# Hybrid encoder trunk: the first two experts' rows come from one-hot products behind the output projection, and the second expert has no gather

## The chip, the cores and the metric

The kernel runs on one core of a Trainium2 chip. The metric is the time of one launch in microseconds on the device. Three runs of the kernel before gave 1538.98, 1540.01 and 1540.28 us.

## The reference

Two layers work on 512 tokens of 1024 numbers in float32. Each layer adds a mixer (eight heads of attention with a forget gate, four heads of retention, then an output projection) and a mixture of experts, and a last RMS norm ends the program. The expert part is what this case is about:

```python
g_idx = argmax(g_logits)                      # one of 4 groups
top_v, top_i = top_k(e_in_group, 2)           # two of its 8 experts
weights = g_w * softmax(top_v)
a = silu(xblk @ w_expert_gate[e]) * (xblk @ w_expert_up[e])
yb = a @ w_expert_down[e]                     # 32 experts, 1024 -> 512 -> 1024
out = segment_sum(yb * w_buf[:, None], tok_buf)
```

Each of the 32 experts has 6.3 MB of weights, so a layer reads some 200 MB for its experts, whatever the tokens choose.

## The kernel before, in words

Each engine has its own program, and the programs meet at semaphores. Up to the router, `steps(layer)` writes out the order of the work by hand, as a list of tuples that PE, ACT and DVE each walk through, doing their own part of each step. `banks()` gives each step a PSUM bank. SP only issues loads of weights; POOL writes the normalised rows to DRAM and issues the gathers.

At the end of the list stands the output projection of four tiles of 128 tokens (t = 0 to 3) in two halves, as `("wp", t, 1, part)` and `("wo", t, half)`. Between its matmuls stand small steps. `fT` transposes half of a tile's residual rows and ACT or DVE copies them from PSUM. `lg` multiplies them with the router weights, and behind its second half DVE runs `choose(layer, t)`: 14 operations, each waiting for the one before, that find the best group, the best expert and the second best, and write a row of `chosen`. `rank` is a product on PE with a triangular matrix that gives each token its place within its expert, which DVE copies and turns into `hot_first`, a one-hot over 64 slots for expert 0. `xb` multiplies this one-hot with the normalised rows `xn2`: the result, in bank 3, are the rows of expert 0, both halves of the width side by side on 64 + 64 partitions. `count` counts the tokens of each expert. `unread` products are written and not read.

Then come 32 experts in a ring of three weight slots. An expert has a gate and an up product (L1774, 32 instructions each), a gated product on DVE, a transpose (L1783), a down product (L1790) and the "spread" (L1750), a one-hot product that adds the weighted results to the tokens and of which DVE adds each part to the residual rows (L1143). The rows of experts 1 to 31 are gathered by POOL from DRAM, by the table `gath`, which is made from `slots_by_expert` (L1486) within expert 0; they are transposed (L1742) within the expert before their own. DVE's `take_input(e)` weighs them with the norm's weights into `xT`. In expert 0 DVE also does `route`, `weigh` and `further`, for the tables.

SP's queue is in order. When the output projection's last step is through, it loads the down weights of expert 0 and up and down of expert 2 (the others are there already). Then it goes through experts 3 to 31: the gate weights wait for the gate product of the expert three before, the up weights for its up product, and the down weights for its down product.

Of the kernel before, what the change touches and what calls it, by code (L numbers as in the profile page):

```python
# [14 lines left out]
P = 128  # L15
# [154 lines left out]
def steps(layer):  # L170
# [62 lines left out]
    out += [("rank", 2), ("fT", 3, 1), ("xb", 2), ("lg", 3, 1), ("rank", 3), ("xb", 3), ("count",)]  # L233
# [7 lines left out]
def banks():  # L241

    acc, uses, where = 0, [0] * 8, {}
    for s in STEPS_OF[0] + [("more",)]:
# [5 lines left out]
        if kind in ("S", "V", "rv"):  # L250
            if kind == "S":
# [18 lines left out]
        elif kind == "RV":  # L270
            b = 6 + s[1] % 2
        elif kind == "RN":
            b = 4 + s[1] % 2
        elif kind == "lg":
            s, b = s[:2], (2, 3, 6, 7)[s[1]]
        elif kind == "fT":
            b = 4 + s[1] % 2
        elif kind in ("rank", "count"):
            b = 2
        elif kind == "xb":  # L280
            s, b = ("xb",), 3
# [20 lines left out]
def trunk_kernel(nc, x, norm_mix_w, w_in, fox_forget_b, w_out, norm_ffn_w, w_router_group, b_router_group,  # L302
                 w_router_expert, b_router_expert, w_expert_gate, w_expert_up, w_expert_down, norm_final_w,
                 const, rope, decay, number, out):
    with ExitStack() as ctx:
# [73 lines left out]
        xg = [at(start, 512) for start in (XF0, XG0, XG0 + 512)]  # L379
        xT = at(XT0, 512).rearrange("p (j h s) -> p j h s", j=4, h=2)  # L380
# [25 lines left out]
        lgt = at(RA0, NT * (NG + NE)).rearrange("p (a b) -> p a b", a=NT)  # L406
        chosen = split("chosen", RA0 + 144, [NT, NE])
        hot_first = [at(RA0 + 304 + t * SLOTS, SLOTS) for t in range(NT - 1)] + [rt(SLOTS)]
        in1, in2, pen, gfi = (at(RA0 + 496 + 4 * i, 4) for i in range(4))
        rank = at(RB2, NT * NE).rearrange("p (a b) -> p a b", a=NT)  # L410
        near, other, o1 = (at(RB2 + 128 + NE * i, NE) for i in range(3))
# [3 lines left out]
        gs = rt(NT, NG)  # L415
# [120 lines left out]
        def gathered(layer, e):  # L536

            count = [len(range(i or 3, NE, 3)) for i in range(3)]
            return 16 * (layer * count[e % 3] + e // 3 + (e % 3 > 0))
# [165 lines left out]
        def _(pool):  # L705
            for layer in range(DEPTH):
# [28 lines left out]
                is_full(pool, ("xb",), layer)  # L735
# [22 lines left out]
                pool.wait_ge(s_xtf, layer * NE + NE - 1)  # L758
# [23 lines left out]
        def _(act):  # L782
# [26 lines left out]
            for layer in range(DEPTH):  # L809
# [13 lines left out]
                for s in STEPS_OF[layer]:  # L823
# [145 lines left out]
                    elif kind == "fT" and s[2] == 0:  # L969
# [3 lines left out]
                                             ).then_inc(freed[b], 2)  # L973
                    if s in UNITS and UNITS.index(s) + CUT < NU:
# [8 lines left out]
                act.wait_ge(s_rin, 2 * layer + 1)  # L983
                nc.scalar.activation(ed, ed, ACT.Exp).then_inc(s_rexp, 1)
                act.wait_ge(s_rin, 2 * layer + 2)
# [43 lines left out]
        def _(dve):  # L1029
# [51 lines left out]
            def choose(layer, t):  # L1081

                g_log, e_log = lgt[:, t, 0:NG], lgt[:, t, NG:].rearrange("p (g e) -> p g e", g=NG)
                gm, top, second = (v[:, t:t + 1] for v in (gmax, m1, m2))
                i1, i2 = in1[:, t:t + 1], in2[:, t:t + 1]
# [12 lines left out]

                link(stt(out=near, in0=o1, scalar=NEG, in1=near, op0=ALU.mult, op1=ALU.add))
# [4 lines left out]
                    ).then_inc(s_hot, 1)  # L1104

            def first_rows(layer):

                for kth, found in enumerate((in1, in2)):
                    link(tt(a12f[:, kth, :, :], over(k("x"), NT), each(found, NE), ALU.is_equal))
                tt(ed, m2, m1, ALU.subtract).then_inc(s_rin, 1)  # L1110
                tt(gs, lgt[:, :, 0:NG], each(gmax, NG), ALU.subtract).then_inc(s_rin, 1)
# [70 lines left out]
            for layer in range(DEPTH):  # L1182
# [5 lines left out]
                for s in STEPS_OF[layer]:  # L1188
# [155 lines left out]
                    elif kind == "fT" and s[2]:  # L1344
# [5 lines left out]
                        if t == NT - 1:  # L1350
                            nc.vector.tensor_copy(wbig, each(nfe[:, layer, :].rearrange("p (h j) -> p j h", h=2), SLOTS))
                    elif kind == "lg" and s[2]:
# [5 lines left out]
                        nc.vector.scalar_tensor_tensor(out=lgt[:, t, :], in0=bank[b][:, 0:NG + NE],  # L1358
# [3 lines left out]
                        choose(layer, t)  # L1362
                    elif kind == "rank":
# [6 lines left out]
                        ts(hot_first[t], k("slot")[:, 0:SLOTS], rank[:, t, 0:1], chosen[:, t, 0:1].bitcast(F32),  # L1370
                           ALU.is_equal, ALU.mult).then_inc(s_first_hot, 1)
# [3 lines left out]
                def take_input(e):  # L1375
                    dve.wait_ge(s_xtf, layer * NE + e + 1)
# [99 lines left out]
        def _(pe):  # L1476
# [50 lines left out]
            for layer in range(DEPTH):  # L1527
                srow = layer * FH * NT
                for s in STEPS_OF[layer]:
# [5 lines left out]
                    elif kind == "xb":  # L1535
                        name, first = ("xb",), s[1] == 0
# [159 lines left out]
                    elif kind == "xb":  # L1696
                        t = s[1]
                        pe.wait_ge(s_xn2, NT * layer + t + 1)
                        pe.wait_ge(s_first_hot, NT * layer + t + 1)
# [7 lines left out]
                    elif kind == "xb":  # L1707
                        done = s[1] == NT - 1
# [22 lines left out]
                def first_transpose():  # L1731
                    b, n = result(("xb",), layer)
                    for j in range(4):
                        if j % 2 == 0:
                            pe.wait_ge(freed[b], 2 * n - 1 + j // 2)
                        last = tr(bank[0][:, P * j:P * (j + 1)], xg[0][:, P * j:P * (j + 1)], ident)
                    last.then_inc(s_xtf, 1)
# [28 lines left out]
                def gate_up(slot, before=None):  # L1766
# [30 lines left out]
                def expert(e):  # L1797
                    i, g = e % RING, layer * NE + e + 1
                    loads = 16 * (layer * per(i) + e // RING + 1)
                    pe.wait_ge(s_xt, g)  # L1800
# [8 lines left out]
                    gate_up(i, ahead).then_inc(s_gu, 1)  # L1809
                    if e == 0:  # L1810
                        weights_by_expert()
# [10 lines left out]
                    if e < NE - 1:  # L1822
# [76 lines left out]
```

## Time and profile before

| | |
|---|---|
| runs | 1538.98, 1540.01, 1540.28 us |
| profiled execution | 1543.27 us, its span 1541.2 us |
| PE, DVE, ACT, POOL busy | 97%, 54%, 24%, 17% of the span |
| mean granted clock of PE | 0.991 |
| HBM | 464.33 MB read, 305 GB/s over the span |

### The profile page before, as it was taken

To read this page: it belongs to the slowest core of one execution; us is meant where nothing else is said; L and a number is where in the kernel's file an instruction comes from. 1 tells how busy PE (TensorE), PEld (TensorE's weight loads), DVE (VectorE), ACT (ScalarE), POOL (GpSimd) and SP (SyncE) were. 2 spreads that over 40 slices of the span, in tenths; PEclk is the share of its full clock that TensorE was granted. 3 is DMA by queue.
4 is the path that set the end of the run, shared out by engine and by line. 5 is a ranking of instruction groups with operands and counts; after the bars stand their busy time and mean duration, and the time that the engine had idled before them with its cause. 6 is when DMAs were issued, how large, how long until landed. Compare 5 with 4: busy or idle time off the path is not lost. (4 is left out here: it accounts for less than half of the span.)

```text
span 1541.2 us, 23569 instructions
## 1 busy us (share of the span) xinstructions
PE 1487.8 (97%) x9368; PEld 931.0 (60%) x9368; DVE 829.7 (54%) x1592; ACT 368.3 (24%) x722; POOL 259.3 (17%) x153
## 2 busy tenths in 40 slices
PE   8999999999999999999999999998999999999996
PEld 6877767655555555545488777685555555554543
DVE  2267773645555555554624686625655555555456
ACT  6335463300000000000163354732000000000002
POOL 3342331110000000000133331501000000000001
PEclk9999999999999999999999999999999999999998
DMA  6442146589999999999833321467999999999995
GB/s 210 99 97 69 42 164 272 202 356 424 421 424 422 423 422 423 423 423 424 338 118 91 82 69 28 173 278 280 391 425 421 425 420 424 421 423 422 425 423 227
DMA packets 105773, 464.05 MB, mean 301 GB/s; under 512 B 16616, under 2 KB 59880, under 8 KB 72640
## 3 DMA queue, kind: packets, MB, share of 16 engines
q1 hardware_dynamic: 98208, 449.14, 73.0%
q0 software_dynamic: 6112, 12.32, 2.1%
q8 instruction: 78, 1.28, 0.3%
q10 hardware_dynamic: 1344, 1.05, 0.2%
q14 instruction: 31, 0.25, 0.0%
HBM read 464.33 MB, written 6.29 MB: 305 GB/s over the span
## 5 line engine op out<-in xcount | busy, mean ns | idle before, releaser
L1774 PE MATMUL bank<-area 128*64 128x256 f32 x4096 | 462.2, 382 | 15.4 <-DMA area<-in_w_expert_up_dram 12.5
L1774 PEld LDWEIGHTS bank<-area 128*64 128x64 f32 x4096 | 289.0, 137 | 182.9 <-issue 26.4
L1143 DVE TENSOR_TENSOR xres<-xres,bank 128x512 f32<-128x512 f32 x512 | 316.6, 681 | 5.3 <-PE bank L1750 5.3
L1790 PE MATMUL bank<-area 128*64 128x512 f32 x1024 | 238.0, 607 | 5.9 <-DVE area L1402 1.0
L744 POOL DMA_INDIRECT area<-rows,gath x62 | 69.9, 1127 | 732.9 <-PE bank L1742 700.0
L995 ACT ACTIVATE y_hi<-bank,slot_w 128x512 fp32r<-128x512 f32 x64 | 44.0, 688 | 586.5 <-PE bank L1790 586.5
L1380 DVE TENSOR_TENSOR area<-area,bank 128x256 f32<-128x256 f32 x64 | 27.0, 421 | 288.3 <-PE bank L1774 288.3
L717 POOL TENSOR_TENSOR w_lo<-area,w_hi 128x1024 fp32r<-128x1024 f32 x55 | 135.1, 2458 | 273.5 <-ACT w_hi L815 273.5
L1790 PEld LDWEIGHTS bank<-area 128*64 128x64 f32 x1024 | 68.9, 138 | 133.9 <-issue 113.3
L1596 PE MATMUL bank<-h_hi,w_hi 128*128 128x512 f32 x336 | 135.0, 402 | 0.0
L1601 PE MATMUL bank<-h_hi,w_lo 128*128 128x512 f32 x320 | 124.9, 390 | 0.0
L1600 PE MATMUL bank<-h_lo,w_hi 128*128 128x512 f32 x320 | 124.7, 390 | 0.0
L1750 PE MATMUL bank<-y_hi,onehot 64*128 64x512 f32 x512 | 115.5, 446 | 3.0 <-issue 1.6
L1750 PE MATMUL bank<-y_lo,onehot 64*128 64x512 f32 x512 | 102.3, 394 | 0.0
L1750 PEld LDWEIGHTS bank<-y_hi,onehot 64*128 64x128 f32 x512 | 48.4, 184 | 83.5 <-issue 75.8
L991 ACT ACTIVATE area<-bank 128x256 f32<-128x256 f32 x64 | 24.5, 383 | 261.5 <-PE bank L1774 261.5
L1384 DVE SCALAR_TENSOR_TENSOR y_lo<-bank,slot_w,y_hi 128x512 fp32r<-128x512 f32 x64 | 48.1, 751 | 62.9 <-ACT y_hi L995 62.8
L815 ACT ACTIVATE w_hi<-area 128x1024 fp32r<-128x1024 f32 x58 | 61.6, 1062 | 80.3 <-PE bank L1524 33.3
L1596 PEld LDWEIGHTS bank<-h_hi,w_hi 128*128 128x128 f32 x336 | 63.0, 188 | 22.9 <-issue 10.3
L1601 PEld LDWEIGHTS bank<-h_hi,w_lo 128*128 128x128 f32 x320 | 60.1, 188 | 13.0
L1600 PEld LDWEIGHTS bank<-h_lo,w_hi 128*128 128x128 f32 x320 | 60.1, 188 | 11.4
L1402 DVE COPY area<-bank 128x256 f32<-128x256 f32 x64 | 27.2, 425 | 67.8 <-PE bank L1783 67.5
(203 smaller groups left out, 1711.1 us busy)
## 6 DMA issues: line engine op xcount, KB each, us to landing
area<-in_w_expert_up_dram SPq DMA_DIRECT2D x64, 2048.0 KB, 25.8
area<-in_w_expert_gate_dram SPq DMA_DIRECT2D x64, 2048.0 KB, 23.5
area<-in_w_expert_down_dram SPq DMA_DIRECT2D x64, 2048.0 KB, 25.1
area<-in_w_in_dram SPq DMA_DIRECT2D x58, 512.0 KB, 3.9
area<-in_w_out_dram SPq DMA_DIRECT2D x4, 2048.0 KB, 11.0
rows<-area POOLq DMA_DIRECT2D x8, 512.0 KB, 3.2
area<-in_decay_dram SPq DMA_DIRECT2D x2, 1024.0 KB, 6.5
out_dram<-area SPq DMA_DIRECT2D x4, 512.0 KB, 2.9
```

The lines of the kernel that those rows point to most:

```text
L717: nc.gpsimd.tensor_tensor(w_lo[g % CUT][:, :, :], slab[g % RAW], w_hi[g % CUT][:, :, :].bitcast(F32), ALU.subtract).then_inc(s_wlo, 1)
L744: pool.indirect_dma_start(out=xg[e % 3], out_offset=None, in_=rows_dram, in_offset=bass.IndirectOffsetOnAxis(ap=gath[:, e:e + 1], axis=0), ...
L815: nc.scalar.activation(w_hi[g % CUT][:, :, :], slab[g % RAW], ACT.Copy).then_inc(s_whi, 1)
L995: nc.scalar.activation(y_hi[e % 2][:, :], bank[3][:, :], ACT.Copy, scale=slot_w[:, e:e + 1]).then_inc(s_yh, 1)
L1143: tt(xs, xs, bank[4 + i][:, :], ALU.add).then_inc(s_sa[i], 1)
L1384: return nc.vector.scalar_tensor_tensor(out=y_lo[e % 2][:, :], in0=bank[found][:, :], scalar=weight, in1=y_hi[e % 2][:, :].bitcast(F32), o ...
L1596: mm(o[:, :], hi[:, c, :], h_hi[:, c, :], start=(c == 0), stop=False)
L1600: mm(o[:, :], hi[:, c, :], h_lo[:, c, :], start=False, stop=False)
L1601: last = mm(o[:, :], lo[:, c, :], h_hi[:, c, :], start=False, stop=(c == KC - 1))
L1750: yield mm(bank[4 + 2 * (t % 2) + half][:, :], onehot[parity][rows, P * t:P * (t + 1)], part[rows, :], start=(w_ == 0), stop=(w_ == 1))
L1774: last = mm(bank[i][SLOTS * half:SLOTS * (half + 1), 0:256], xT[:, c % 4, c // 4, :], w[:, i, c, 256 * half:256 * (half + 1)], start=(c == ...
L1790: last = mm(bank[into][SLOTS * half:SLOTS * (half + 1), :], hx[:, c % 2, c // 2, :], w[:, c, 512 * half:512 * (half + 1)], start=(c == 0), ...
```

## The change

The one-hot of a tile now has 128 columns: 64 slots of expert 0 and 64 of expert 1. `xb` makes two products with it, one for each half of the width, into banks 3 and 6. All four `xb` steps now stand behind the output projection. DVE copies the first result and ACT the second into `two_rows`, four transposes turn each (banks 5 and 7), and `take_input(0)` and `take_input(1)` make their input from these banks, in two products of 256 columns each. Expert 0's gate product starts when the first is there, and waits for the second at its fifth chunk. Expert 1 has no gather and no transposes within expert 0, and POOL gathers expert 2 first, then 3 and 4 as soon as the first transposes are done. The slot table is made behind expert 0's up product, not ahead of it. `choose` is split into nine and five operations with one more (a subtraction for the softmax over groups, which was one operation for all tiles); for tile 2 the second part stands behind the copy of `fT(3, 1)`. `rank(2)` stands behind the last logits, one `unread` product is gone, and in the first part the logits of tiles 0 to 3 stand a step later. The buffers `lgt`, `near`, `o1`, `gs` share or change places.

The diff, cut to its core (the second places of buffers and the gathers' semaphore counts are left out):

```diff
-    out += [("wo", 0, 0), ("wo", 1, 0), ("fT", 0, 0), ("wo", 2, 0), ("fT", 1, 0), ("lg", 0, 0)]
-    out += [("wo", 3, 0), ("fT", 2, 0), ("lg", 1, 0)]
-    between = [[("fT", 3, 0), ("lg", 2, 0)], [("lg", 3, 0)], []]
+    out += [("wo", 0, 0), ("wo", 1, 0), ("fT", 0, 0), ("wo", 2, 0), ("fT", 1, 0), ("wo", 3, 0), ("lg", 0, 0), ("fT", 2, 0)]
+    between = [[("lg", 1, 0), ("fT", 3, 0)], [("lg", 2, 0)], [("lg", 3, 0)]]
     for t in range(1, NT):
-        between += [[("fT", t - 1, 1)],
-                    [("rank", t - 2), ("lg", t - 1, 1)] if t > 1 else [("lg", t - 1, 1)],
-                    [("xb", t - 2)] if t > 1 else []]
+        between += [[("fT", t - 1, 1)], [("rank", t - 2), ("lg", t - 1, 1)] if t > 1 else [("lg", t - 1, 1)], []]
     for n, small in enumerate(between):
         out += [("wp", n // 3, 1, n % 3), *small]
         if n % 3 == 2:
             out += [("wo", n // 3, 1)]
-    out += [("rank", 2), ("fT", 3, 1), ("xb", 2), ("lg", 3, 1), ("rank", 3), ("xb", 3), ("count",)]
+    out += [("xb", 0), ("fT", 3, 1), ("xb", 1), ("lg", 3, 1), ("rank", 2), ("rank", 3), ("xb", 2), ("xb", 3), ("count",)]
...
+                made = {0: [(("xb", 0), 3), (("xb", 1), 6)], 3: [(("xt", 0), 5), (("xt", 1), 7)]}.get(s[1], [])
...
-        hot_first = [at(RA0 + 304 + t * SLOTS, SLOTS) for t in range(NT - 1)] + [rt(SLOTS)]
...
+        hot_two = [at(start, 2 * SLOTS) for start in (RA0 + 216, RA0 + 344, RB2 + 128)] + [rt(2 * SLOTS)]
...
-                is_full(pool, ("xb",), layer)
+                is_full(pool, ("xb", 0), layer)
...
-                for e in range(1, RING):
-                    gather(e)
+                gather(2)
                 for e in range(RING, NE):
-                    pool.wait_ge(s_xtf, layer * NE + e - RING + 1)
+                    if e == RING:
+                        is_full(pool, ("xt", 0), layer)
+                    elif e - RING >= 2:
+                        pool.wait_ge(s_xtf, block_turned(layer, e - RING))
...
+                    elif s == ("xb", NT - 1):
+                        b, n = result(("xb", 1), layer)
+                        is_full(act, ("xb", 1), layer)
+                        nc.scalar.activation(two_rows[1], bank[b][:, :], ACT.Copy).then_inc(freed[b], 2)
...
+            def choose_second(layer, t):
...
+                ts(gs[:, t, :], lgt[:, 0:NG], gmax[:, t:t + 1], None, ALU.subtract).then_inc(s_rin, 1)
...
-                b, n = result(("xb",), layer)
-                is_full(dve, ("xb",), layer)
-                for half in range(2):
-                    own = slice(256 * half, 256 * (half + 1))
-                    nc.vector.tensor_copy(xg[0][:, own], bank[b][:, own]).then_inc(freed[b], 1)
+                b, n = result(("xb", 0), layer)
+                is_full(dve, ("xb", 0), layer)
+                nc.vector.tensor_copy(two_rows[0], bank[b][:, :]).then_inc(freed[b], 2)
...
+                            choose_second(layer, t - 1)
...
-                        choose(layer, t)
+                        choose_first(layer, t)
+                        if t != NT - 2:
+                            choose_second(layer, t)
...
-                        ts(hot_first[t], k("slot")[:, 0:SLOTS], rank[:, t, 0:1], chosen[:, t, 0:1].bitcast(F32),
-                           ALU.is_equal, ALU.mult).then_inc(s_first_hot, 1)
+                        for e in range(2):
+                            ts(hot_two[t][:, SLOTS * e:SLOTS * (e + 1)], k("slot")[:, 0:SLOTS], rank[:, t, e:e + 1],
+                               chosen[:, t, e:e + 1].bitcast(F32), ALU.is_equal, ALU.mult).then_inc(s_first_hot, 1)
...
+                    if e < 2:
+                        for h in range(2):
+                            b, n = result(("xt", h), layer)
+                            is_full(dve, ("xt", h), layer)
+                            found = bank[b][:, :].rearrange("p (j s) -> p j s", j=4)[:, :, SLOTS * e:SLOTS * (e + 1)]
+                            made = tt(xT[:, :, h, :], found, wbig[:, :, h, :], ALU.mult)
+                            if e == 0 or h:
+                                made.then_inc(s_xt, 1)
+                            else:
+                                link(made)
+                        if e:
+                            dve.wait_ge(s_xt, input_part(layer, e))
+                            for h in range(2):
+                                dve.sem_inc(freed[result(("xt", h), layer)[0]], 2)
+                        return
...
-                            last = mm(o[SLOTS * half:SLOTS * (half + 1), :], hot_first[t],
-                                      xn2[t][:, 512 * half:512 * (half + 1)], start=(t == 0), stop=(t == NT - 1))
+                            to = result(("xb", half), layer)[0]
+                            last = mm(bank[to][:, :], hot_two[t], xn2[t][:, 512 * half:512 * (half + 1)],
+                                      start=(t == 0), stop=(t == NT - 1))
+                            if t == NT - 1:
+                                last.then_inc(full[to], 1)
...
-                        unread(0, 512, 512, 512, 512)
+                        unread(0, 512, 512, 512)
...
+                        may_fill(pe, ("xt", h), layer)
+                        is_taken(pe, ("xb", h), layer)
+                        for j in range(4):
+                            last = tr(bank[b][:, P * j:P * (j + 1)], two_rows[h][:, P * j:P * (j + 1)], ident)
+                        last.then_inc(full[b], 1)
...
+                            if parts and i == 0 and c == 4:
+                                pe.wait_ge(s_xt, input_part(layer, 0))
...
-                        if part and e == 0:
-                            slots_by_expert()
...
+                        slots_by_expert()
                         weights_by_expert()
...
-                    if e < NE - 1:
+                    if 0 < e < NE - 1:
```

## Rows read from the trace of the kernel before

**Rows 1.** Windows of the expert phases: busy us by engine, clock, DMA share, GB/s.
```profile
321.00:329.00 8.00, 8.00 (x50) 3.71 (x48) 6.88 (x20) 0.72 (x2) 0.29 (x1) 0.78 0.43 120
329.00:760.00 431.00, 422.06 (x3122) 232.29 (x3120) 226.56 (x397) 33.77 (x62) 30.68 (x27) 1.00 1.01 422
...
1069.00:1072.00 3.00, 3.00 (x28) 2.09 (x26) 0.35 (x2) 0.38 (x1) 0.00 (x0) 1.00 0.54 104
...
1083.00:1088.00 5.00, 5.00 (x42) 2.81 (x40) 4.62 (x13) 0.90 (x2) 0.00 (x0) 1.00 0.65 191
```

**Rows 2.** SP's issues in time: start us, us, engine, line, operation.
```profile
291.63 0.38 SPq L607 DMA_DIRECT2D area<-in_w_expert_down_dram  x1
...
325.51 0.38 SPq L607 DMA_DIRECT2D area<-in_w_expert_down_dram  x1
...
1084.33 0.38 SPq L607 DMA_DIRECT2D area<-in_w_expert_down_dram  x1
```

**Rows 3.** PE in time, layer 0; in brackets idle before and releaser.
```profile
280.60 1.08 PE L1701 MATMUL bank<-area 128*64 128x512 f32 x4
...
284.51 0.60 PE L1674 MATMUL bank<-kst,xres 128*128 128x128 f32 x4
...
291.44 0.34 PE L1691 MATMUL bank<-chosen,sums 128*128 128x32 f32 x2
...
295.32 3.68 PE L1499 MATMUL bank<-kst 128*128 128x512 f32 x8
...
302.00 0.62 PE L1695 MATMUL bank<-chosen,sums 128*128 128x32 f32 x4
...
304.14 3.67 PE L1774 MATMUL bank<-area 128*64 128x256 f32 x32 [0.78 <-DVE area L1377]
...
312.35 1.97 PE L1493 MATMUL bank<-area,hot_slot 128*128 128x32 f32 x16
314.15 0.42 PE L1783 MATMUL bank<-kst,area 128*128 128x128 f32 x2
318.18 1.12 PE L1742 MATMUL bank<-kst,area 128*128 128x128 f32 x4 [3.61 <-DMA area<-rows,gath]
319.22 6.24 PE L1790 MATMUL bank<-area 128*64 128x512 f32 x16
...
335.37 3.65 PE L1790 MATMUL bank<-area 128*64 128x512 f32 x16
```

**Rows 4.** PE in time, the same place in layer 1.
```profile
1050.94 0.34 PE L1691 MATMUL bank<-chosen,sums 128*128 128x32 f32 x2
...
1060.49 1.08 PE L1701 MATMUL bank<-area 128*64 128x512 f32 x4 [0.84 <-DVE area L1370]
...
1064.07 5.88 PE L1774 MATMUL bank<-area 128*64 128x256 f32 x32 [0.79 <-DVE area L1377]
```

**Rows 5.** Windows of one microsecond, layer 1, columns as in Rows 1.
```profile
1061.00:1062.00 1.00, 1.00 (x8) 0.50 (x4) 0.55 (x4) 0.88 (x3) 0.29 (x1) 0.88 0.95 348
...
1068.00:1069.00 1.00, 1.00 (x10) 0.66 (x8) 0.00 (x0) 0.00 (x0) 0.00 (x0) 0.71 0.95 401
```

**Rows 6.** DVE in time, layer 0: choice, projection's add, one-hot, first 256-wide product.
```profile
282.68 0.25 DVE L1103 SCALAR_TENSOR_TENSOR chosen<-kst,area 128x32 fp32r<-128x32 f32 x1
283.39 0.69 DVE L1339 TENSOR_TENSOR xres<-xres,bank 128x512 f32<-128x512 f32 x1 [0.46 <-PE bank L1668]
...
299.17 0.25 DVE L1103 SCALAR_TENSOR_TENSOR chosen<-kst,area 128x32 fp32r<-128x32 f32 x1
...
300.53 0.32 DVE L1370 TENSOR_SCALAR area<-kst,area,chosen 128x64 f32<-128x64 f32 x1
...
304.00 0.41 DVE L1052 TENSOR_TENSOR area<-area 128x256 f32<-128x256 f32 x1
```

**Rows 7.** The page's table of DMA queues.
```profile
q0 software_dynamic: 6112, 12.32, 2.1%
```

**Rows 8.** The source view of the gathers, line 744.
```profile
DMA to landing us min/median/max: 3.9/8.2/11.0
```

More of the change, by code:

```diff
@@ L379, in trunk_kernel @@
         xg = [at(start, 512) for start in (XF0, XG0, XG0 + 512)]
+        two_rows = [at(XF0 + i * 512, 512) for i in range(2)]
         xT = at(XT0, 512).rearrange("p (j h s) -> p j h s", j=4, h=2)
@@ L404, in rt_one_pass @@
             return split(name, start, list(shape))
-        lgt = at(RA0, NT * (NG + NE)).rearrange("p (a b) -> p a b", a=NT)
-        chosen = split("chosen", RA0 + 144, [NT, NE])
-        hot_first = [at(RA0 + 304 + t * SLOTS, SLOTS) for t in range(NT - 1)] + [rt(SLOTS)]
-        in1, in2, pen, gfi = (at(RA0 + 496 + 4 * i, 4) for i in range(4))
+        chosen = split("chosen", RA0, [NT, NE])
+        lgt = at(RA0 + 128, NG + NE)
+        in1, in2, pen, gfi = (at(RA0 + 168 + 4 * i, 4) for i in range(4))
+        other = at(RA0 + 184, NE)
         rank = at(RB2, NT * NE).rearrange("p (a b) -> p a b", a=NT)
-        near, other, o1 = (at(RB2 + 128 + NE * i, NE) for i in range(3))
+        hot_two = [at(start, 2 * SLOTS) for start in (RA0 + 216, RA0 + 344, RB2 + 128)] + [rt(2 * SLOTS)]
+        near, gs = slot_w[:, 0:NE], slot_w[:, NE:NE + NT * NG].rearrange("p (a b) -> p a b", a=NT)
+        o1 = slot_tok[:, 0:NE]
+        assert NE + NT * NG <= NCOL
         gmax, m1, m2 = (stat[:, 20 + 4 * i:24 + 4 * i] for i in range(3))
@@ L536, in gathered, with block_turned, input_part @@
         def gathered(layer, e):
-            count = [len(range(i or 3, NE, 3)) for i in range(3)]
-            return 16 * (layer * count[e % 3] + e // 3 + (e % 3 > 0))
+            first = (RING, RING + 1, 2)[e % RING]
+            return 16 * (layer * len(range(first, NE, RING)) + (e - first) // RING + 1)
+        def block_turned(layer, e):
+            return layer * (NE - 2) + e - 1
+        def input_part(layer, e):
+            return layer * (NE + 1) + e + 2
         def spread_use(layer, e, t):
@@ L757, in _ @@
                 n_more = pool.value_load(ovn[0:1, 0:1], min_val=0, max_val=NOV)
-                pool.wait_ge(s_xtf, layer * NE + NE - 1)
+                pool.wait_ge(s_xtf, block_turned(layer, NE - 1))
                 with pool.If(n_more > 0):
@@ L1079, in slot_weights, with choose_first @@
                 dve.sem_inc(s_wt, 1)
[L1081 to L1085, printed above, removed]
+            def choose_first(layer, t):
+                g_log, e_log = lgt[:, 0:NG], lgt[:, NG:].rearrange("p (g e) -> p g e", g=NG)
+                gm, top, i1 = gmax[:, t:t + 1], m1[:, t:t + 1], in1[:, t:t + 1]
                 stt = nc.vector.scalar_tensor_tensor
@@ L1097, in choose @@
                 link(ts(o1, k("x"), i1, None, ALU.is_equal))
+            def choose_second(layer, t):
+                second, i2 = m2[:, t:t + 1], in2[:, t:t + 1]
+                stt = nc.vector.scalar_tensor_tensor
                 link(stt(out=near, in0=o1, scalar=NEG, in1=near, op0=ALU.mult, op1=ALU.add))
@@ L1357, in _ @@
                         dve.wait_ge(s_rstd2, layer * NT + t + 1)
-                        nc.vector.scalar_tensor_tensor(out=lgt[:, t, :], in0=bank[b][:, 0:NG + NE],
+                        if t:
+                            dve.wait_ge(s_rin, (NT + 1) * layer + t)
+                        nc.vector.scalar_tensor_tensor(out=lgt, in0=bank[b][:, 0:NG + NE],
                                                        scalar=stat[:, 16 + t:17 + t], in1=rtb[:, layer, :],
@@ L1535, in _ @@
                     elif kind == "xb":
-                        name, first = ("xb",), s[1] == 0
+                        name, first = ("xb", 0), s[1] == 0
                     elif kind == "begin":
@@ L1707, in _ @@
                     elif kind == "xb":
-                        done = s[1] == NT - 1
+                        done = False
                     elif kind in ("begin", "wp"):
@@ L1731, in first_transpose @@
                 def first_transpose():
[L1732 to L1737, printed above, removed]
+                    for h in range(2):
+                        b, n = result(("xt", h), layer)
+                        may_fill(pe, ("xt", h), layer)
[3 more added lines that the diff above has]
+                        last.then_inc(full[b], 1)
                 def input_transpose(e):
@@ L1764, in spread_block, with gate_up @@
                             made[2 + half].then_inc(s_sf[2 * (t % 2) + half], 1)
-                def gate_up(slot, before=None):
+                def gate_up(slot, before=None, parts=False):
                     w = wexp[slot][0]
@@ L1807, in ahead @@
                         pe.wait_ge(s_w[i][part], loads)
-                    gate_up(i, ahead).then_inc(s_gu, 1)
+                    gate_up(i, ahead, e == 0).then_inc(s_gu, 1)
                     if e == 0:
+                        slots_by_expert()
                         weights_by_expert()
```

22 lines of the change are left out of this document (10 added, 12 removed).

## The prediction

> **What bounds the kernel now.** I read first the windows over both expert phases. [rows 1] show the weight stream: once it runs it holds a DMA share of 1.01 and 422 to 423 GB/s, to 760 in layer 0 and alike in layer 1, which is the rate at which these phases end; PE is never short of work there by more than a little. So what a change ahead of the stream is worth is read from the stretches in which DMA isn't full: 321 to 329 (120 GB/s, so 8 x (1 - 120/422) = 5.7 us lost), 1069 to 1072 (104 GB/s, 2.3 us) and 1083 to 1088 (191 GB/s, 2.7 us). Then SP's issues [rows 2]: three loads go out from 291.63 on, when the output projection is through, the gate weights of expert 3 when expert 0's gate product ends (304.14 + 3.67, [rows 3]), and its down weights only at 325.51, when expert 0 has left its slot. From that issue nothing is dry again. Full rate comes some 1.9 us after an issue (effective start 327.4: 321 + 5.7, and 0.7 for the transfers of a gather that lie in this gap). Third, PE's order in time [rows 3] says why 325.51: PE starts expert 0 at 304.14 (I call this E0), has turned its hidden rows at 314.5, and then stands 3.61 us for the gathered rows of expert 1, after which the down product takes 6.24 us, against 3.65 us in the next expert, since the granted clock stood at 1.2 GHz. Layer 1 is 759.5 us later at the end of the output projection (1050.94 against 291.44), starts expert 0 at 1064.07 with a gate product of 5.88 us at 1.2 GHz, waits again for gathered rows, and issues down weights at 1084.33 [rows 2, 4, 5]. In both layers the distance E0 to this issue is long: 21.4 and 20.3 us.
>
> **The projection's end.** Two one-hot products (xb) leave it: one at 280.60 and one like it in the next tile, each 1.01 us and 0.1 us of waiting, 2.2 us of PE in all [rows 3]. DVE gives some back. The choice of a tile gets one more 4-wide subtraction (about 0.17 us), and the add of the projection stands behind it. At 283.39 this add waited 0.46 us for PE, with the choice over at 282.93; with two such subtractions ahead the choice ends at 283.3, and DVE becomes the bound there: the add comes at 283.3, so removing the first xb brings fT(2,1), four transposes, only from 284.51 to 284.15 [rows 3, 6]. From there PE is free: 0.36 + 1.11 = 1.5 us earlier, W = 289.95. DVE's choice there is cut after its ninth of 14 operations (2.1 us of 3.35) and ends at 289.7, just in time. Bounds: 0.4 us (the DVE keeps all else) and 2.2 us. The second expert's one-hot is one more 64-wide operation per tile, 0.32 us, 0.17 if it overlaps; DVE waits about that long for the next logits just behind it, which hides it; without that cover 0.3 us a tile [rows 6]. SP's three loads at 291.63 go out 1.5 us earlier as well. The logits moved behind wo(3,0) swap 0.9 us of PE work within a stretch in which no load is short; zero, and 0.3 us either way if not.
>
> **From W to E0.** An xb is now two products of 128 columns instead of two of 64. The trace has no such xb; the nearest row is the four unread 512-wide ones, 8 instructions in 3.68 us, so 0.92 us each, 1.84 us for a pair. The lower end is the 1.01 us of the pair of 64, the upper end twice 1.84 at the low clock; I take 1.84. PE then: xb(0) 289.95 to 291.9, fT(3,1) 0.4, xb(1) to 294.2, logits 0.92 to 295.15, three unread ones (2.76, one fewer) to 297.9, rank(2) 0.4. All of it but the logits' end at 295.15 is beside DVE's chain: the choice of tile 3 took from 295.32 (end of logits) to 299.42, 4.1 us [rows 3, 6], so it ends at 299.25. The five late operations of tile 2 (1.2 us) and the copy for the weights stand at 292.9 to 294.8, before the logits, in DVE idle time: no cost, but a price of up to 1.2 us if the logits come sooner. Then what was not there: DVE's subtraction, the copy of rank(2) and its release (0.6 us), since rank(3) uses the same bank. rank(3) 299.85 to 300.45; xb(2), xb(3) 3.7 us, which wait for four one-hots of 0.32 us made during rank(3), to 304.3; count 0.6; four transposes 0.4 (fT: the next work starts 0.35 after them); the first of two 256-wide products on DVE 0.42 [rows 3, 6] and 0.2 of signals: E0 = 305.7, against 304.14. The copy of the first half (0.69 us) lies beside the second half of xb(3) and the count; ACT's copy of the second half, if it takes as long, ends beside the count and the first transposes; the second product on DVE is needed 1.8 us after E0 and is done by then. The move puts 1.6 us onto E0; bounds 0 and 4.5 us. In layer 1 E0 = 1050.94 - 1.5 + 15.75 = 1065.2.
>
> **From E0 to the down weights.** Gate and up 7.2 us; the slot table, now behind both, 1.0; the weight table 1.85; hidden transposes and the copy back 1.1 (hidden transposes at 314.15; the same step takes that long in the next expert); down 3.65: 14.85 us, issue at 320.55 and 1080.05 [rows 3]. The wait for the gather is gone, and so is the low clock that followed it. DVE waits for the table at E0 + 8.3 ahead of its gated product; this ends at E0 + 9.2, and the weight table on PE runs until E0 + 10.05, which hides it. On POOL's queue gather(2) is now first, then 3 and 4 at once. gather(2) is issued at E0 + 9.6, lands 8.2 us later, at worst 11.0 [rows 8], so by E0 + 21.7, and PE asks for it at E0 + 24.4, one expert on: nothing waits. What is late next? The gate weights of expert 3: issued at E0 + 3.7, full rate at + 5.6, two loads 4.19 MB / 423 GB/s = 9.9 us and three gathers of 0.13 MB each (12.32 MB of this queue less 4.2 MB for the saved rows, over 62 [rows 7, 8]) 0.9 us: E0 + 16.4, against 14.85 + 1.9 = E0 + 16.75 for the down weights. So both end nearly together, and the down weights still decide.
>
> **Sum.** Layer 0: 325.51 - 320.55 = 4.95. Layer 1: 1084.33 - 1080.05 = 4.3. One gather fewer in a stream that is full: 0.13 MB, 0.3 us, twice. 9.85 us in all with the clock full. PE has the same 4.95 and 4.3 us, so its waits for weights don't grow.
>
> **The clock.** [rows 4, 5] against [rows 3]: with the same work the granted clock fell to 1.2 GHz at 1061.8 in layer 1 (the mean of that microsecond is 0.88), after waits of at most 0.84 us, and did not in layer 0. The fall lasted to 1068.6 and made the gate product 5.88 instead of 3.67 us and the transposes 0.3 longer: 2.5 us. After the change PE waits 1.5 us in one piece (298.3 to 299.85) at this place, in both layers, so I expect what the trace shows, a fall in one of two: 9.85 - 2.5 = 7.35. The Trainium skill (TensorE: Matmul & The Clock Gate, HAM oscillation) ties such falls to waits for data far longer than these; by that rule there is no fall ahead of E0 and the sum is 9.85. By that rule the fall at 1061.8 should not be there, so the trace doesn't agree.
>
> The profiled execution took 1543.27 us (span 1541.2 and 2.07 around it), 3.26 above the median 1540.01. 1543.27 - 7.35 = 1535.9 in its terms, 1532.7 in the median's.
>
> **Rivals.** (a) Forecast, 0.45: 1532.7. (b) No fall ahead of either E0, 0.27: 1540.01 - 9.85 = 1530.2. For: layer 0; against: longer wait than in layer 1. (c) A fall in both layers for the 6.8 us that it lasted at 1061.8 to 1068.6, each 3.4 us of lost work on products that fill PE: 9.85 - 6.8 = 3.05, 1537.0; 0.2. For: the wait is there in both; against: the 3.7 us of full products that follow it. (d) Slower, 0.08: PE stays at 1.2 GHz from W on, because four one-hot products of double width and only three unread ones change what the clock sees. The work from W to E0 on PE is 13.8 us, of which DVE's chain hides some 3: 10.7 us more per layer. Break-even is where E0 slips by 6.5 us in layer 0 (21.4 - 14.85) and 5.4 in layer 1, that is with 13 and 11 us of low clock; then 2 x 10.7 - 9.85 = 11.5 slower, 1551.6. Against: before W PE is full, and the longest fall seen ahead of experts is 6.8 us. (e) That the gain is hidden by another wait, as that for gather(2), needs a landing 2.7 us above the largest of 62; I fold it into (c).
>
> **Chances.** Some 0.2% (3.1 us) is what a measurement tells from no change. Half of (c) counts as within it: faster 0.82, within 0.12, slower 0.06. The range goes from (b) less the bounds of the projection's end (0.7 us in each layer), 1528.8, to (c) and half a microsecond, 1537.5; slower cases are left out.
>
> **What would show it.** Right: no wait for gathered rows in expert 0; down product 3.65 us there; last projection product 1.5 us sooner; E0 1.6 us later counted from the layer's start in layer 0; down weights of expert 3 out at 320.6 in layer 0; between 308 and 311 a new dry stretch of DMA of up to 3 us, and after 323 none. Wrong: E0 later than 308, an xb pair of more than 2 us at full clock, a wait at input_transpose(2), or a stream that is full as early as said and an end that does not follow it.

## The result, and the profile after

The changed kernel took 1530.94 us (median of 10 runs, 1529.91 to 1537.1), the kernel before 1540.32 in the same comparison (10 runs, 1538.98 to 1544.58): ratio 0.9941, 95% interval 0.9929 to 0.9952, so 9.1 us less, at least 7.4. A second comparison of the two gave 1532.53 (6 runs) against 1540.35, ratio 0.9942 (0.9928 to 0.9956). The forecast was 1532.7 within 1528.8 to 1537.5. The profiled execution took 1530.88 us, span 1529.0.

PE in time in layer 0, to be read beside [rows 3] (start us, us, engine, line, operation, idle before and its releaser):

```profile
287.60 1.88 PE L1739 MATMUL bank<-area 128*128 128x512 f32 x4
289.31 0.60 PE L1709 MATMUL bank<-kst,xres 128*128 128x128 f32 x4
289.75 1.88 PE L1739 MATMUL bank<-area 128*128 128x512 f32 x4
291.47 0.98 PE L1717 MATMUL bank<-rtw,area 128*128 128x36 f32 x8
292.28 2.82 PE L1534 MATMUL bank<-kst 128*128 128x512 f32 x6
...
296.52 0.51 PE L1726 MATMUL bank<-chosen,sums 128*128 128x32 f32 x3 [1.18 <-DVEq L1388]
...
297.24 3.67 PE L1739 MATMUL bank<-area 128*128 128x512 f32 x8
...
302.31 7.13 PE L1817 MATMUL bank<-area 128*64 128x256 f32 x64
...
313.15 3.65 PE L1833 MATMUL bank<-area 128*64 128x512 f32 x16 [0.67 <-DVE area L1437]
```

The wait for the gathered rows is gone, and the down product is 3.65 us. The projection's end, W, is where the first pair of 128-column products starts: 287.60 against 291.44. Expert 0's gate product, E0, starts at 302.31 against 304.14: earlier, where I had it 1.6 us later. Layer 1 ends its expert 0 otherwise:

```profile
1055.04 7.13 PE L1817 MATMUL bank<-area 128*64 128x256 f32 x64
1062.10 1.06 PE L1521 MATMUL bank<-hot_exp,hot_slot 128*128 128x32 f32 x8
1063.02 1.95 PE L1528 MATMUL bank<-area,hot_slot 128*128 128x32 f32 x16
1064.80 0.41 PE L1826 MATMUL bank<-kst,area 128*128 128x128 f32 x2
1065.89 6.67 PE L1833 MATMUL bank<-area 128*64 128x512 f32 x16 [0.67 <-DVE area L1437]
```

From the end of the projection up to the down product the granted clock is 1.00 in both layers; then the down product of layer 1 runs at 0.50, and takes 6.67 us where that of layer 0 took 3.65. SP's issues, beside [rows 2]:

```profile
287.79 0.38 SPq L615 DMA_DIRECT2D area<-in_w_expert_down_dram  x1
...
306.03 0.33 SPq L607 DMA_DIRECT2D area<-in_w_expert_gate_dram  x1
...
316.85 0.38 SPq L615 DMA_DIRECT2D area<-in_w_expert_down_dram  x1
...
991.96 0.34 SPq L607 DMA_DIRECT2D area<-in_w_expert_gate_dram  x1
...
1072.60 0.38 SPq L615 DMA_DIRECT2D area<-in_w_expert_down_dram  x1
```

And the windows of the stretches in which the stream is not full, in the columns of [rows 1]:

```profile
306.00:308.00 2.00, 2.00 (x22) 1.32 (x20) 0.50 (x2) 0.39 (x1) 0.00 (x0) 1.00 0.63 135
308.00:310.00 2.00, 2.00 (x20) 1.33 (x16) 0.00 (x0) 0.00 (x0) 0.00 (x0) 1.00 0.87 352
...
316.00:320.00 4.00, 4.00 (x36) 2.42 (x34) 3.62 (x12) 0.69 (x1) 0.00 (x0) 1.00 0.98 384
1056.00:1061.00 5.00, 5.00 (x50) 3.34 (x48) 3.10 (x10) 0.39 (x1) 0.00 (x0) 1.00 0.84 282
1065.00:1072.00 7.00, 6.33 (x18) 1.80 (x18) 6.09 (x18) 0.00 (x0) 2.62 (x3) 0.51 0.91 380
1071.00:1075.00 4.00, 4.00 (x32) 2.12 (x30) 3.76 (x9) 0.69 (x1) 0.00 (x0) 0.88 0.49 127
```

Where the time of layer 0 came from can be read off these: the three loads go out 3.84 us earlier (291.63 to 287.79), and the dry stretches cost 2 x (1 - 135/422) + 2 x (1 - 352/422) + 4 x (1 - 384/422) = 2.05 us where 321 to 329 cost 5.7. That is 7.5 us, and layer 1's first load goes out 7.4 earlier (999.40 before, 991.96 after). The issue of the down weights itself is 8.66 us earlier; the last 1.3 us of that are not passed on, for the stream by then also pauses behind the gate weights' issue (306 to 310). In layer 1 the own part is 3.2 us of earlier loads (1051.13 to 1040.52, less 7.4) and 5.0 us of dry stretches against 1.7 + 2.8 = 4.5: 3.7 us. The second of these stretches comes with the slow down product, which held the slot: in a kernel below whose down product took 3.65 us it is gone. Together 11.1 of the 12.4 us between the two profiled executions; that of before stood 3 us above its median.

### The profile page after: what moved, and what is told of

Same layout as the page of the kernel before. It is cut to its first block and busy times, and to the rows that moved or that the text cites. A ratio compares the mean times of both kernels' runs of the same rounds, so it can differ in the third digit from the quotient of the medians.

```text
span 1529.0 us, 23597 instructions
## 1 busy us (share of the span) xinstructions
PE 1482.5 (97%) x9364; PEld 932.9 (61%) x9364; DVE 828.2 (54%) x1608; ACT 369.4 (24%) x724; POOL 257.5 (17%) x151
```

## The experiments

All medians below are against the runs of the kernel before on the same chip. Two readings of the gain stand against each other. Theory: the changed kernel's gain is the removed gather wait with its low clock, and the one-hot products out of the projection; the order of the logits counts for nothing. Rival: it is PE's small waits within the projection, the order of the logits above all. Neither alone will do, as the runs show.

**The logits' order alone**, on the kernel before:

```diff
-    out += [("wo", 0, 0), ("wo", 1, 0), ("fT", 0, 0), ("wo", 2, 0), ("fT", 1, 0), ("lg", 0, 0)]
-    out += [("wo", 3, 0), ("fT", 2, 0), ("lg", 1, 0)]
-    between = [[("fT", 3, 0), ("lg", 2, 0)], [("lg", 3, 0)], []]
+    out += [("wo", 0, 0), ("wo", 1, 0), ("fT", 0, 0), ("wo", 2, 0), ("fT", 1, 0), ("wo", 3, 0), ("lg", 0, 0), ("fT", 2, 0)]
+    between = [[("lg", 1, 0), ("fT", 3, 0)], [("lg", 2, 0)], [("lg", 3, 0)]]
```

> The kernel before with one edit: the first half's logits stand one step later, as in the changed kernel (the xb steps, gathers and choice are untouched). Theory A: this part of the change, which I had priced at nothing, takes three waits of PE for the copy between fT and lg (about 0.55 us each) off the projection in each layer, so the last projection product, expert 0 and the down weights of expert 3 all come 1.7 us sooner and the time falls by 3.4 us, to a ratio of 0.998. Rival: the order is worth nothing (0 +- 0.6 us), and the extra gain came from the xb steps leaving the projection.

1539.98 us, ratio 0.9996 (0.9988 to 1.0005): no difference can be told. **The same order put back in the changed kernel:**

> The changed kernel with the old order of the first half's logits. Theory A: 3.4 us slower than the changed kernel, the fT-to-lg waits back in the profile, some 6 us faster than before. Rival: as fast as the changed kernel, 9.4 us faster than before.

1536.27, ratio 0.9972 (0.9962 to 0.9982). Without the new order the changed kernel loses 4 to 5 us, half of its gain. In this trace the last two pairs of one-hot products of layer 0 also ran in part at 1.2 GHz (5.37 us for 3.67), so not all of the loss need be the order's. PE's first part of the projection, from the transposes of tile 0 to the first of the second half, in three traces. Before:

```profile
252.61 0.60 PE L1674 MATMUL bank<-kst,xres 128*128 128x128 f32 x4
...
255.45 1.08 PE L1682 MATMUL bank<-rtw,area 128*128 128x36 f32 x8 [0.41 <-DVE xres L1339]
...
258.85 1.08 PE L1682 MATMUL bank<-rtw,area 128*128 128x36 f32 x8 [0.41 <-DVE xres L1339]
...
268.98 0.60 PE L1674 MATMUL bank<-kst,xres 128*128 128x128 f32 x4
```

The changed kernel:

```profile
251.98 0.60 PE L1709 MATMUL bank<-kst,xres 128*128 128x128 f32 x4
...
255.63 0.97 PE L1717 MATMUL bank<-rtw,area 128*128 128x36 f32 x8
...
266.91 0.60 PE L1709 MATMUL bank<-kst,xres 128*128 128x128 f32 x4
```

The changed kernel with the old order:

```profile
251.72 0.60 PE L1710 MATMUL bank<-kst,xres 128*128 128x128 f32 x4
...
254.56 1.08 PE L1718 MATMUL bank<-rtw,area 128*128 128x36 f32 x8 [0.41 <-DVE xres L1354]
...
268.09 0.60 PE L1710 MATMUL bank<-kst,xres 128*128 128x128 f32 x4
```

From the first transposes to those of the second half: 16.37 us, 14.93, and 16.37 again, with the same products in between. The old order makes PE wait twice, 0.41 us each as the rows show, and costs 1.44 us in all. The releaser in the brackets is not the copy of the transposed rows, as the expectation above has it, but DVE's add of a projection product. `banks()` says why: the logits of tile 0 are written to bank 2, and those of tile 1 to bank 3, where the projection products of tiles 2 and 3 had just been made, and DVE must add these to the residual rows first. DVE and ACT in the kernel before:

```profile
254.71 0.69 DVE L1339 TENSOR_TENSOR xres<-xres,bank 128x512 f32<-128x512 f32 x1 [1.13 <-PE bank L1668]
...
258.10 0.69 DVE L1339 TENSOR_TENSOR xres<-xres,bank 128x512 f32<-128x512 f32 x1 [2.71 <-PE bank L1668]
...
256.38 0.58 ACT L972 ACTIVATE area<-bank 128x512 f32<-128x512 f32 x1
```

The adds end at 255.40 and 258.79, and the logits start at 255.45 and 258.85. The copy for the second logits (the ACT row) had ended at 256.96. One step later in the order, the add is over before the logits ask for the bank. The rows ahead of the prediction don't reach this stretch.

**The first one-hot products behind the last logits**, on the kernel before (64 columns, gather kept):

```diff
-                    [("xb", t - 2)] if t > 1 else []]
+                    []]
...
-    out += [("rank", 2), ("fT", 3, 1), ("xb", 2), ("lg", 3, 1), ("rank", 3), ("xb", 3), ("count",)]
+    out += [("rank", 2), ("fT", 3, 1), ("lg", 3, 1), ("xb", 0), ("xb", 1), ("xb", 2), ("rank", 3), ("xb", 3), ("count",)]
...
-                        unread(0, 512, 512, 512, 512)
+                        unread(0, 512)
```

> The kernel before with only this edit: xb(0) and xb(1), still of 64 columns, stand behind the last logits with xb(2), in the place of three of the four unread products. Theory A: the last projection product comes 1 us sooner (DVE's unsplit choices hold the rest), expert 0 and the down weights of expert 3 too, so 2 us faster than before. Rival: DVE's choices hold all of it, 0 +- 0.6 us.

1538.52, ratio 0.9987 (0.9978 to 0.9995), 1.7 to 2 us. **Both edits together:**

> The kernel before with both: the new order of the logits, and the first two one-hot products (64 columns, expert 0 alone) behind the last logits; the second expert's gather stays and is waited for. Alone the first was worth 0.4 us and the second 1.8, though in the changed kernel the order is worth 4 to 5 us. Theory A, the order counts wherever the stretch ahead of the experts is PE's, and needs the one-hot products out of it: 1534.5 to 1536 us, the projection's end 3.2 us earlier than before. Theory B, the wait for the gather (and the low clock behind it) takes back what comes earlier, whatever comes earlier: 1537.5 to 1539 us.

1537.58, ratio 0.9978 (0.9967 to 0.9988): near the edge of theory B. The distance from tile 0's first transposes to the projection's end (the start of what follows it, less its wait) shows how closely the two parts add, in layer 0: before 291.44 - 252.61 = 38.83; order 37.35 (-1.48); products out 36.95 (-1.88); both 35.52 (-3.31); the changed kernel 287.60 - 251.98 = 35.62 (-3.21), with the old order 37.07 (-1.76). Layer 1 gives the same: 38.99 before, 37.58, 37.12 and 35.72. So PE's path gets 3.3 us shorter in each layer of the last experiment, and the time falls by 3.1 for both layers together. PE in time there, layer 0 and layer 1:

```profile
313.49 0.93 PE L1741 MATMUL bank<-kst,area 128*128 128x128 f32 x4 [2.76 <-DMA area<-rows,gath]
314.35 5.02 PE L1789 MATMUL bank<-area 128*64 128x512 f32 x16
...
1044.89 1.92 PE L1681 MATMUL bank<-rtw,area 128*128 128x36 f32 x8 [0.85 <-DVE area L1347]
...
1048.60 3.97 PE L1700 MATMUL bank<-area 128*64 128x512 f32 x12
...
1070.11 1.12 PE L1741 MATMUL bank<-kst,area 128*128 128x128 f32 x4 [2.57 <-DMA area<-rows,gath]
1071.15 5.50 PE L1789 MATMUL bank<-area 128*64 128x512 f32 x16
```

The wait for the gather stays: 2.76 and 2.57 us, in sum the 5.3 us of before (3.61 and 1.69). The down product behind it stays slow, 5.02 and 5.50 us, and in layer 1 a stretch at the low clock stands ahead of the experts (eight logits products in 1.92 us, where other rows have 0.98). Over all runs the mean granted clock is 0.9934 to 0.9939 for the kernel before in these comparisons, 0.9918 with the order, 0.9910 with the products out, 0.9898 with both (11 to 20 runs each), against 0.994 in the changed kernel. 0.004 of 1540 us is 6 us of PE's work, so in these kernels, which keep the wait for the gather, what comes earlier and the loss of clock are of one size. That the one pays for the other is argued from this and not shown, and why these kernels get less clock is not settled.

**The wait for the gather alone.** Two kernels on the changed one: the slot table back between gate and up, and with that a gather of expert 1 that PE waits for (its rows aren't used; the semaphore counts and a wait on POOL's side are left out):

```diff
+                gather(1)
...
+                    if e == 0:
+                        pe.wait_ge(s_gat[1], gathered(layer, 1))
```

> The changed kernel with the slot table made between expert 0's gate and up product again. Theory A: the down weights of expert 3 are issued at the same distance from the start of expert 0 (14.5 us), the up weights 1 us later while the gate weights still run, so within 0.5 us of the changed kernel. Rival: the table between the products delays the stream by its 1.0 us in each layer, 2 us slower.

> As the run with the table back, and POOL gathers expert 1's rows again, which nobody reads, and PE waits for them behind expert 0's hidden transposes as before. Theory A: the wait is 3 to 4 us, with or without a fall of the clock behind it that adds up to 2.6 us; the down weights of expert 3 go out 4 to 6 us later in each layer, so 8 to 12 us slower than the run with the table back: most of the gain is gone. Rival: the gate weights of expert 3 bind the stream anyway, and the wait costs no more than 2 us.

Table back: 1532.92, ratio 0.9943 (0.993 to 0.9956), the changed kernel's own ratio; no effect of its place can be told, and in layer 1, where none of expert 0's products is slow, the distance from E0 to the down weights' issue is 14.79 us against the changed kernel's 14.54. With the wait: 1536.13, ratio 0.9969 (0.9957 to 0.9981), 3.2 us more. The waited-for kernel, layer 0:

```profile
313.32 0.41 PE L1829 MATMUL bank<-kst,area 128*128 128x128 f32 x2
315.61 5.00 PE L1836 MATMUL bank<-area 128*64 128x512 f32 x16 [1.87 <-DMA area<-rows,gath]
```

The wait is 1.87 us here and 1.40 in layer 1, and the down products take 5.00 and 5.27. Of each wait 0.67 us stands there without the gather too (the wait for the copy of the hidden rows), so the gather lengthens PE's path by 1.2 and 0.7 us, 1.9 of the 3.2 measured. The rest is not separated: the mean granted clock is 0.9933 over the 6 runs with the wait and 0.9950 over the 5 without, which is 2.6 us of PE's work, and one gather more per layer goes through the stream. A slow down product comes without the gather too: the kernel with the table back had one of 5.35 us in layer 0, and of 3.65 in layer 1. I had priced a wait of 3.61 us, and the difference of 6.24 to 3.65 with it. This kernel does not put back that whole price, since its rows are there sooner: the product that waits for them starts 6.3 us after the gather (issued at 309.30), against 8.1 in the kernel before (310.12 and 318.18).

**The choice in two parts.** With tile 2's choice whole again:

> The changed kernel with tile 2's choice in one piece again. Theory A: DVE's add of the last projection product comes 0.9 us later, but PE has xb(0) to do there until 289.3, so the transposes behind it slip by 0.3 us and the five operations left behind them are gone from the time ahead of the last logits: 0 to 0.6 us slower per program. Rival: the split is what lets the logits come early, 1.2 us per layer, 2.4 us slower.

1532.07, ratio 0.9948 (0.9935 to 0.9961). The trace shows what the split avoids: PE waits 0.26 us at `fT(3, 1)` in layer 0, and the path from W to E0 is 0.45 us longer. That is below what the runs can tell.

**The low clock in expert 0's down product.** First, unread products in the 0.67 us ahead of it:

```diff
+                    if e == 0:
+                        unread(3, 256)
```

> The changed kernel with one unread product of 256 columns behind expert 0's hidden transposes, in the 0.67 us in which PE waits for the copy there. Theory A: the clock falls there in some executions because the narrow products of the tables come just before; the filler makes such falls rarer, so 0 to 1.5 us faster in the median and a narrower spread. Rival: the narrow products alone do it, no change.

1530.2, ratio 0.9938 (0.9922 to 0.9954), which cannot be told from the changed kernel. The wait is 0.24 us and the down product still 5.24 us in layer 0 (3.65 in layer 1): a wait of 0.67 us is not needed for a slow one. **Then another order:** the last logits ahead of the first two pairs of one-hot products, with unread products in the two short waits this opens. The edit does two things more: the three unread products behind the logits are gone (the unread products of this stretch have 896 columns in all, where those of the changed kernel have 1536), and DVE's copy of the norm's weights moves behind tile 3's choice (not shown below).

```diff
-    out += [("xb", 0), ("fT", 3, 1), ("xb", 1), ("lg", 3, 1), ("rank", 2), ("rank", 3), ("xb", 2), ("xb", 3), ("count",)]
+    out += [("fT", 3, 1), ("lg", 3, 1), ("xb", 0), ("xb", 1), ("rank", 2), ("rank", 3), ("xb", 2), ("xb", 3), ("count",)]
...
-                    if s == ("lg", NT - 1, 1):
+                    if s == ("wo", NT - 1, 1):
...
-                        unread(0, 512, 512, 512)
+                        unread(0, 512)
+                    if s == ("fT", NT - 1, 1):
+                        unread(0, 384)
```

> A version that ought to beat both kernels: the last transposes and logits stand ahead of xb(0) and xb(1), with an unread product of 512 and one of 384 columns in PE's waits and none behind the logits, and the copy of the norm's weights moves behind tile 3's choice. Theory A: the time from the last projection product to expert 0 is DVE's chain from the last logits on, which start 1.4 us sooner, so expert 0 starts 1.4 us sooner and the time falls by 2.8 us below the changed kernel. Rival: PE's products are the bound of this stretch (their sum is unchanged), no change; or the clock falls ahead of expert 0, some us slower.

1529.77 (1528.08 to 1530.11), ratio 0.993 (0.9917 to 0.9943). To tell it from the changed kernel, both once more on one chip, and with the unread products of the experiment above:

> The changed kernel once more, for the spread of the comparison itself. Every theory: ratio 0.993 to 0.995 to the kernel before (1529.9 to 1532), and the same places in the trace: down-projection weights of layer 0 issued at 316.8 (to 0.5 us), of layer 1 at 1072.6 (to 1 us). Open is whether expert 0's down products in layer 1 are 6.7 us again: if the clock's fall there is the sequence's own (narrow table products, then 0.67 us of wait), they are over 5 us again; if it is chance, 3.65.

> The last logits ahead of the first two experts' rows, once more, beside the changed kernel on the same chip. If the 1.2 us between the two were the shorter way from the projection's end to expert 0 (14.1 for 14.7 us, twice), it is 1 to 2 us below the changed kernel in this call too; if they were scatter, the two medians lie within 0.7 us of each other.

> The last logits ahead of the rows, and unread products of 256 columns in the wait ahead of expert 0's down products. If the wait of 0.67 us there is what brings the clock down, both layers' down products are 3.65 us and the time is 1 to 3 us below the changed kernel, with less scatter; if the fall has no tie to that wait, the same time as without the filler, to 0.7 us, and some down products over 5 us.

The changed kernel 1532.53 (1529.93 to 1533.29), ratio 0.9942 (0.9928 to 0.9956); logits first 1528.24 (1526.58 to 1530.21), 0.9917 (0.9903 to 0.9932); with unread products 1527.59 (1526.99 to 1528.59), 0.9912 (0.9898 to 0.9927). The last lies below both kernels with intervals that don't meet: 4.9 us below the changed one, 12.8 below the one before. PE in its layer 0:

```profile
296.31 0.51 PE L1726 MATMUL bank<-chosen,sums 128*128 128x32 f32 x3 [0.90 <-DVEq L1388]
...
302.10 7.13 PE L1819 MATMUL bank<-area 128*64 128x256 f32 x64
...
312.95 3.65 PE L1835 MATMUL bank<-area 128*64 128x512 f32 x16 [0.23 <-DVE area L1437]
```

From W (287.97) to E0 it is 14.13 us, 0.58 less than in the changed kernel, and 13.72 in layer 1, 0.99 less: 1.6 us. The rest of the 4 to 5 us goes with the clock, whose mean over the runs is 0.9942 in the changed kernel and 0.9960 and 0.9962 in the two with the logits first. The traces show where: with the one-hot products first and no gather to wait for, 9 of 12 down products of expert 0 took 5 us or more (two layers in each of six traces), for instance both in the changed kernel's second trace:

```profile
313.27 5.24 PE L1833 MATMUL bank<-area 128*64 128x512 f32 x16 [0.67 <-DVE area L1437]
...
1066.77 5.35 PE L1833 MATMUL bank<-area 128*64 128x512 f32 x16 [0.67 <-DVE area L1437]
```

With the logits first none of six did. The edit changes the order and the unread products together, so which of them does it is not shown. In that version the second dry stretch of layer 1 is gone, where the changed kernel had 127 GB/s from 1071 to 1075 (windows of the second trace of logits first, without the added unread products):

```profile
1065.00:1072.00 7.00, 7.00 (x56) 3.78 (x54) 6.45 (x19) 1.07 (x2) 1.09 (x1) 1.00 0.97 399
1071.00:1075.00 4.00, 4.00 (x40) 2.59 (x35) 2.71 (x7) 0.38 (x1) 0.00 (x0) 1.00 1.03 434
```

**What the runs add up to.** In the changed kernel putting back the order of the logits costs 4 to 5 us and putting back a wait for the gather 3.2; in the kernel before, the order is worth 0.4 and the one-hot products out of the projection 1.7 to 2. PE's distances add up within 0.1 us. The times do not add up, and the mean granted clock differs between these kernels.

## Why the prediction was right, and where it was not

The sign, the places and nearly the size were right. The size came out partly by luck, by two errors of opposite sign: a path that got shorter by 3.1 us more in each layer than forecast, and a price per microsecond that was too high.

- **The projection's end.** Forecast 1.5 us from the two one-hot products, measured 1.76 in the changed kernel with the old order. Right.
- **The logits' order.** Priced at zero, 0.3 either way; it is 1.45 us in each layer. This is the term that was most mis-sized. The cost lay in two waits of 0.41 us for a bank that DVE had still to empty, and what I took for a swap of equal work took them away.
- **W to E0.** Forecast 15.75 us, measured 14.71. Nearly the whole difference stands ahead of `rank(3)`: a pair of 128-column products takes 1.71 us from start to next start, not 1.84 to 1.95, the logits 0.81, the choice ends 3.9 us behind them and not 4.1, and PE's wait is 1.18 us and not 1.5. From `rank(3)` to E0 it is 5.79 us, forecast 5.85. (The terms that I wrote down for this piece add up to 305.9, not 305.7.)
- **E0 to the down weights.** Forecast 14.85, measured 14.54; what goes last is still the down product. The latest landing of gather(2), E0 + 21.7, was a wrong sum: 9.6 + 11.0 is 20.6, which leaves 3.8 us of room and not 2.7. Nothing hangs on it, as PE did not wait there.

These, with the 0.63 us by which this trace starts its projection earlier, explain 316.85 against the 320.55 that I forecast: 0.63 + 1.45 + 0.26 + 1.04 + 0.31 = 3.69.

- **What an earlier issue is worth.** Here the error of the other sign. With the measured path my sum would have grown from 9.85 to 9.85 + 2 x 3.06 = 16 us. The two profiled executions differ by 12.4: of layer 0's 8.66 us only 7.4 arrived, and layer 1's slow down product took 3.0 us more than I had for it, together a little more than the 3.6 us in question. The medians differ by 9.4, 3 us less again, since I took the low clock of one profiled execution as what the kernel always pays: that execution stood at 0.991 and 1543.27, while the runs of before have means of 0.993 to 0.994 and a median of 1540.3. The gather's wait and the clock behind it, 6.2 us in layer 0 by [rows 3], were 1.69 + 1.55 us in layer 1, a number that I had not put down.
- **The clock.** I expected one fall ahead of E0 in two layers. There was none in either trace of the changed kernel, as rival (b) had it. Two of the other four kernels traced with this order of products had one, in one layer each: 5.37 us for 3.67 at the last two pairs of one-hot products (the old order of the logits, layer 0; the table back, layer 1). So a fall ahead of E0 was not ruled out, only rarer than one in two layers; in its place expert 0's down product ran at the low level in three of four layers of the changed kernel, which cost 3.0 us in layer 1 of the first trace. Its time, 1530.94, is nearer to (b), 1530.2, than to the forecast, but not by (b)'s mechanism of a clock that stays full.
- **What else was to be seen.** No wait at the next expert's input: right. Dry stretch of up to 3 us: it is 306 to 310, 1.7 us lost, where I had 308 to 311. None after 323: right in layer 0, wrong in layer 1 (1071 to 1075, which is 16 to 20 us behind E0, where 323 is 17.3 behind the E0 of my forecast).

In the five traces with a wait of 1.4 to 3.6 us for gathered rows, all ten down products behind it were slow; yet nine of twelve were slow behind a wait of 0.67 or 0.24 us as well, and none of six behind the same waits after other products some twenty microseconds earlier. The rule of the Trainium skill (TensorE: Matmul & The Clock Gate, HAM oscillation) ties falls to waits for data longer than most of these, so it does not account for them. What decides it stays open; 16 narrow products (128x32, 1.95 us) stand ahead of the down product in all of them.

## What to carry to other kernels

Before a step is priced at nothing because only its place changes, read the rows on both sides of its old place for a wait of the same engine, and look up which bank the step writes and who has still to read it: the wait may be what the move takes away. Compare the clock of the profiled execution with that of the runs before its low stretches are booked as gain, for a kernel whose path gets shorter can show a lower clock and gain less than the path says. And where the clock falls in one place in some executions and not in others, filling the wait in front of it may not help (5.24 us behind 0.24 us of wait); another arrangement of the work ahead of it is worth a run.

## What was not expected of the hardware

Two edits that together shorten PE's path by 3.3 us in each of two layers shortened the time by 3.1 us, with the mean granted clock down from 0.9938 to 0.9898 on the same chip and runs between 1532.8 and 1540.43. And a down product behind the same wait of 0.67 or 0.24 us took 5.06 to 6.67 us in nine of twelve layers with the one-hot products first, and 3.65 us in six of six with the logits first and fewer unread products, an edit some twenty microseconds ahead of it. Six layers from three traces are few, and which half of the edit does it was not tried.
